# A fourth pair of projection chunks in seven block products, and the gate products in another slot of a sparse-attention layer

## What is computed

```python
h = rmsnorm(x, g_norm)                       # x: 256 x 2048
proj = einsum('bsd,de->bse', h, w_in)        # 2048 -> 4*1024 + 2*1024 + 6*256 + 24 columns
(m_q, m_k, m_v, m_z, n_q, n_kc, n_vc, n_ks, n_vs, n_kw, n_vw, n_g, n_z) = split(proj)
...
q_rot = apply_rope(nq, cos, sin)             # the gated heads' queries, rotated
q_raw = nq                                   # and raw: they meet the compressed keys
k_c = compress_tokens(n_kc, pe_ck, w_ck1, w_ck2)    # silu(flat @ w1) @ w2
v_c = compress_tokens(n_vc, pe_cv, w_cv1, w_cv2)
gates = sigmoid(n_g)                         # three gates per gated head
o_nsa = nsa_attention(q_rot, q_raw, k_c, v_c, k_s, v_s, k_w, v_w, gates)
y = concat([rmsnorm(o_moba * silu(m_z)), rmsnorm(o_nsa * silu(n_z))])
return x + einsum('bse,ed->bsd', y, w_out)
```

## Time and profile before

| | |
|---|---|
| median of 3 runs | 496.52 us (496.51 to 496.88) |
| the profiled execution, its own time | 496.67 us |
| its span (first to last instruction) | 494.9 us |
| around the span | 1.77 us |
| granted TensorE clock, mean | 0.997 |
| PE / DVE / ACT / POOL busy | 98% / 71% / 52% / 13% |
| HBM read and written | 93.93 MB and 2.10 MB |

### The profile page before, as it was taken

How to read it: one execution, slowest core, us unless ns; L and a number is a source line. 1 busy time by engine, 2 the same in 40 slices (tenths; PEclk the granted TensorE clock), 3 DMA queues, 4 the chain that set the end, 5 groups by cost and what they waited for, 6 DMA issues and landing times.

```text
span 494.9 us, 6495 instructions
## 1 busy us (share of the span) xinstructions
PE 485.8 (98%) x2506; PEld 404.2 (82%) x2506; DVE 352.1 (71%) x554; ACT 256.7 (52%) x368; POOL 64.2 (13%) x66
## 2 busy tenths in 40 slices
PE   8999999999999999999999999999999999999993
PEld 7888788787788888888888888888888888888882
DVE  5886643445879958776587887766898879888643
ACT  5884335353556535645444455664665546466422
POOL 2350101000202202000020200000313231040120
PEclk9999999999999999999999999999999999999998
DMA  8989788685454552533544724448247769643304
GB/s 293 329 285 378 248 301 298 200 281 179 148 182 159 166 174 88 170 121 136 171 134 164 255 59 158 141 150 303 85 136 267 277 244 310 230 152 116 140 1 170
DMA packets 54576, 96.45 MB, mean 195 GB/s; under 512 B 4401, under 2 KB 13201, under 8 KB 54161
## 3 DMA queue, kind: packets, MB, share of 16 engines
q1 hardware_dynamic: 54512, 96.03, 57.0%
q10 hardware_dynamic: 32, 0.01, 0.0%
HBM read 93.93 MB, written 2.10 MB: 194 GB/s over the span
## 4 chain that ended last, share of the span: by engine, by line
PE 96%; issue 1%; DMA 1%; DVE 0%; ACT 0%; ACTq 0%; POOLq 0%; POOL 0%; DVEq 0%
PE proj L677 26%; PE proj L679 26%; PE proj L678 26%; PE b_o L974 4%; PE b_t L658 2%; PE b_p L943 2%; PE b_s L843 2%; PE proj L710 2%; PE proj L716 1%; PE proj L721 1%; DMA xo<-in_x_dram 1%; PE b_s L679 1%; PE b_s L677 1%; PE b_s L678 1%; PE b_p L658 0%
## 5 line engine op out<-in xcount | busy, mean ns | idle before, releaser
L1391 DVE TENSOR_TENSOR w_lo<-w_raw,w_hi 128x2048 fp32r<-128x2048 f32 x67 | 155.3, 2320 | 74.6 <-ACT w_hi L1053 74.4
L677 PE MATMUL proj<-w_hi,xT_hi 128*128 128x512 f32 x500 | 197.1, 394 | 0.0
L679 PE MATMUL proj<-w_hi,xT_lo 128*128 128x512 f32 x500 | 195.0, 390 | 0.0
L678 PE MATMUL proj<-w_lo,xT_hi 128*128 128x512 f32 x500 | 194.8, 390 | 0.0
L1053 ACT ACTIVATE w_hi<-w_raw 128x2048 fp32r<-128x2048 f32 x67 | 127.9, 1912 | 27.5 <-PE proj L679 17.0
L677 PEld LDWEIGHTS proj<-w_hi,xT_hi 128*128 128x128 f32 x500 | 93.9, 188 | 20.8 <-issue 1.6
L679 PEld LDWEIGHTS proj<-w_hi,xT_lo 128*128 128x128 f32 x500 | 93.8, 188 | 20.0
L678 PEld LDWEIGHTS proj<-w_lo,xT_hi 128*128 128x128 f32 x500 | 94.0, 188 | 18.5
L1199 ACT ACTIVATE pT<-b_p 128x512 f32<-128x512 f32 (+2 forms) x24 | 11.8, 490 | 53.9 <-PE b_p L943 53.9
L625 POOL TENSOR_TENSOR rope_a<-rope_a,rope_b 128x512 f32<-128x512 f32 (+1 forms) x12 | 13.1, 1108 | 160.8 <-DVE rope_b L1478 160.8
L677 PE MATMUL proj<-w_hi,ymT_hi 128*128 128x512 f32 x70 | 27.3, 390 | 0.0
(11 more groups left out here) (252 smaller groups left out, 562.9 us busy)
## 6 DMA issues: line engine op xcount, KB each, us to landing
w_raw<-in_w_in_dram SPq DMA_DIRECT2D x53, 1024.0 KB, 5.1
w_raw<-in_w_out_dram SPq DMA_DIRECT2D x14, 1024.0 KB, 5.1
xo<-in_w_ck_dram SPq DMA_DIRECT2D x4, 1024.0 KB, 7.8
xo<-in_w_cv_dram SPq DMA_DIRECT2D x4, 1024.0 KB, 7.8
w_raw<-in_w_in_dram SPq DMA_DIRECT2D x12, 256.0 KB, 6.5
Q<-in_x_dram SPq DMA_DIRECT2D x1, 2048.0 KB, 10.1
out_dram<-Q SPq DMA_DIRECT2D x8, 256.0 KB, 2.8
xo<-in_x_dram SPq DMA_DIRECT2D x3, 512.0 KB, 7.6
```

Source lines behind the costliest of these rows:

```text
L677: nc.tensor.matmul(dst, a_hi, b_hi, start=first, stop=False, skip_group_check=goes_on)
L678: nc.tensor.matmul(dst, a_hi, b_lo, start=False, stop=False, skip_group_check=goes_on)
L679: return nc.tensor.matmul(dst, a_lo, b_hi, start=False, stop=last, skip_group_check=goes_on)
L1391: nc.vector.tensor_tensor(wl, w_raw[:, u % RAW], wh.bitcast(F32), ALU.subtract).then_inc(lo_ready, 1)
```

## The change

The two `nq` chunks (3 and 4) become the first pair of four. Their seven block products are spread over slots 10 to 13, and slot 18 has no unit of its own any more. The four fp32 weight blocks and three of the four half-done copies lie in `Q`, where the fp32 transposed x was: so the gates' products, which read it, move from slot 13 to slot 4 (their sums to slot 5, on all engines), and SP waits for them before it loads two of the blocks. The raw queries are finished by DVE (`nq_sums`) and not by ACT. The later pairs keep their slots.

```diff
-PAIRS = [(11, 12), (13, 14), (NC + 2, NC + 3)]
+PAIRS = [(3, 4), (11, 12), (13, 14), (NC + 2, NC + 3)]
+FIRST_BLOCKS, T2_SLOT, EARLY = [8, 40, 48, 65], [10, 41, 49, 66], [10, 42, 50, 66]
+MIDDLE_BLOCKS, LATE_BLOCKS = [11, 42, 50, 67], [12, 43, 51, 68]
+MIDDLE, LATE = [12, 44, 52, 68], [13, 45, 53, 69]
...
+ROUNDED_AT = {9: 10, 10: 11, 11: 12, 12: 13, 13: 14, 14: 15, 15: 16, 17: 17,
...
-CK_LOAD = [6, 7, 11, 12, 14, 15, 17, 18]
+CK_LOAD = [6, 7, 11, 12, 13, 14, 16, 17]
-GATE_SLOT = 13
+GATE_SLOT = 4
...
+                if u == 8:
+                    block(NQ_PAIR, 0)
+                if u == 10:
+                    sp.wait_ge(gates_done, 1)
+                    block(NQ_PAIR, 1)
+                    block(NQ_PAIR, 3)
+                if u == 12:
+                    sp.wait_ge(xs_lo_ok, 1)
+                    block(NQ_PAIR, 2)
...
-                if kv:
-                    pe.wait_ge(gate_exp, 2)
+                pe.wait_ge(gate_exp, 2)
...
-                if slot == 40:
-                    xs_round()
+                if slot in (7, 40):
+                    xs_round((7, 40).index(slot))
...
                     if slot == MIDDLE[p]:
-                        if p == 2:
+                        if p in (NQ_PAIR, OUT_PAIR):
                             block_hi(p, 4)
                             block_hi(p, 5)
                         mid_out_(p, 2)
...
+            def nq_sums(i):
+
+                n = CHUNKS[i][2]
+                dve.wait_ge(unit_used, used_by_chunk(i))
+                dve.wait_ge(mid_out, 4)
+                if n:
+                    dve.wait_ge(t_round, rounds_by(UPC * i + UPC - 1))
+                copies = [mid_copy(NQ_PAIR, c) for c in ((0, 3) if n else (2, 1))]
+                for m in range(MT):
+                    nc.vector.scalar_tensor_tensor(raw_e[:, m, :], proj_b[i % 2][m][:, :], rstd[:, m:m + 1], copies[m],
+                                                   ALU.mult, ALU.add).then_inc(dve_read, 1)
...
-                if slot == 38:
-                    x_sums()
-                if slot == 40:
-                    xs_residual()
+                if slot in (6, 38):
+                    x_sums((6, 38).index(slot))
+                if slot in (8, 40):
+                    xs_residual((8, 40).index(slot))
```

More of the change, by code:

```diff
@@ L75, in plain @@
         units.append((c, g))
[L77 to L93, removed]
+    starts = {pair[0]: p for p, pair in enumerate(X_PAIRS)}
+    for c in range(NC):
+        p = PAIR_OF.get(c)
+        for g in range(UPC):
+            if g == (2 if p is None else 3) and c + 1 in starts:
+                ring.append(("early", starts[c + 1]))
+            if p is None or g:
+                if c in starts and g < 3:
+                    ring.append((("middle", "late")[g - 1], p))
+                plain(c, g)
     for c, g in OUT_UNITS[:-1]:
         plain(NC + c, g)
-    a, b = PAIRS[2]
-    ring.append(("early", 2))
+    a, b = PAIRS[OUT_PAIR]
+    ring.append(("early", OUT_PAIR))
     plain(NC + OUT_UNITS[-1][0], OUT_UNITS[-1][1])
-    ring.append(("middle", 2))
+    ring.append(("middle", OUT_PAIR))
     plain(a, 1)
-    ring.append(("late", 2))
+    ring.append(("late", OUT_PAIR))
     for c, g in ((a, 2), (a, 3), (b, 1), (b, 2), (b, 3)):
@@ L122, in unit_at @@
 def unit_at(slot):
-    for p, (a, b) in enumerate(PAIRS[:Z_PAIRS]):
+    for p, (a, b) in enumerate(X_PAIRS):
         s0 = MIDDLE[p]
@@ L127, in unit_at @@
             return {2: UNIT_NO[a, 2], 3: UNIT_NO[a, 3], 4: UNIT_NO[b, 1], 5: UNIT_NO[b, 2], 7: UNIT_NO[b, 3]}.get(slot - s0)
[L128 to L136, removed]
+    a, b = PAIRS[OUT_PAIR]
+    late = LATE[OUT_PAIR]
+    if slot >= MIDDLE[OUT_PAIR]:
+        return {late + 1: UNIT_NO[a, 2], late + 2: UNIT_NO[a, 3], late + 3: UNIT_NO[b, 1]}.get(slot)
+    if slot >= NPROJ:
+        c, g = OUT_UNITS[slot - NPROJ]
+        return UNIT_NO[NC + c, g]
+    return UNIT_NO[slot // UPC, slot % UPC]
+ROUNDED_AT = {9: 10, 10: 11, 11: 12, 12: 13, 13: 14, 14: 15, 15: 16, 17: 17,
+              41: 40, 42: 41, 43: 42, 44: 43, 45: 44, 46: 45, 47: 46, 49: 47, 50: 48, 52: 49, 53: 50, 54: 51, 55: 52, 56: 53, 57: 54, 58: 55,
+              66: 61, 67: 62, 68: 63, 69: 64, 70: 65, 71: 66, 72: 67}
 def rounded_at(slot):
-    if slot < 40:
+    if slot < 8:
         return slot + 2
-    return slot - 2 if 60 <= slot < 65 else ROUNDED_AT.get(slot)
+    if 18 <= slot < 40:
+        return slot
+    return slot - 4 if 60 <= slot < 65 else ROUNDED_AT.get(slot)
 OUT_SLOT = [OUT_DONE[0], OUT_DONE[1] + 1, OUT_DONE[2]]
@@ L1003, in _ @@
                 for p in range(len(PAIRS)):
-                    if slot == EARLY[p] and p < Z_PAIRS:
+                    if slot == EARLY[p] and p != OUT_PAIR:
                         pair_early(p)
@@ L1360, in _ @@
                     act.wait_ge(gates_sum, 1)
+                    act.wait_ge(rstd_ok, 2)
                     for m in range(MT):
@@ L1788, in _ @@
                         block_lo(p, 1)
-                    if slot == MIDDLE_BLOCKS[p] and p:
+                    if slot == MIDDLE_BLOCKS[p] and p != Z1:
                         block_lo(p, 2)
```

237 lines of the change are left out of this document (124 added, 113 removed).

## The result

The changed kernel takes **499.78 us** (median; its four executions: 499.14, 498.89, 500.42 and 500.52) against 496.69 before: a ratio of 1.0062, 95% interval 1.0049 to 1.0075. That is 3.1 us slower. The forecast was 498.7, with 497.0 to 500.2 as its range. The profiled execution took 499.14 with a span of 497.3, 2.4 above the span of before.

A forecast was written before the change was run, and what follows sets the result against it. PE was taken as the bound, busy 485.8 of 494.9 us. The profiled 496.67 - 1.36 (products) + 1.05 (slots 10 to 13) + 2.45 (slot 18) = 498.81, 0.15 above the median, so 498.7; range 497.0 to 500.2.

The forecast's parts named there:

- Six products, -1.36: Pair of chunks: 42 block products replace 48, six fewer at 0.227 us each, -1.36 us on PE.
- The rival of blocks that switch buffers: Pair's blocks: more frequent buffer switches eat into the six products' gain, 0.2 us at most; no chance of its own.
- Gates moved, 0: Slots 13 and 14 to 4 and 5: PE does the gates' 16 products, 1.73 us, in either place; cost 0.
- Early part, 0: Slots 6 to 10: some 8 us of added DVE work and smaller DMA pieces cost PE nothing.
- Slots 10 to 13, +1.05: Longer ACT and DVE queues make PE wait before P7 (0.6 to 0.7), then 0.25 and 0.15; ends 0 and 2.2.
- Slot 18, +2.45: Second layer directly behind the MLP's sums waits for `hid_ready`: 2.37 us formerly hidden by a unit, plus 0.1 waking.
- the collision: Slot 18: hidden's first DVE step takes 1.11 us beside POOL's addition; without it 0.9 less (rivals 0.10 and 0.07).
- After slot 18, no wait: Slots 19 and 20 onward: PE is nearer to ACT and DVE, yet waits for nothing; cost 0.
- 3.1 us nearer: Slots 19 and 20: second layer begins 2.45 us behind the sums, not 5.54, bringing PE closer to ACT and DVE.
- The clock, 0.03: Rival: slot 18's wait brings on a stretch at granted clock 0.88, costing 1.5 us more, 500.2; chance 0.03.

The follow-up runs named there:

- the half unit and the later sum: Changed kernel with half of slot 19's unit moved into slot 18 before the second layer, and DVE's fourth block sum moved from slot 11 to 12: 497.51 us, ratio 1.0015.
- the half unit: Changed kernel with slot 19's unit cut in two, its first half in slot 18 between the MLP's sums and second layer: 498.69 us, ratio 1.0041.
- the gates alone: Kernel before with only the gates' products and small steps moved from slots 13 and 14 to 4 and 5: 496.81 us, ratio 1.0006.
- the earlier rounding: Changed kernel with ACT's and DVE's rounding of slot 19's unit one slot earlier, in slot 16: 498.52 us, ratio 1.0040.
- the wait alone: Kernel before with only the values' second layer in slot 18 placed ahead of the unit, directly behind the MLP's sums: 500.96 us, ratio 1.0080.
- the best version: Changed kernel with the half unit, later fourth sum, earlier rounding, two more units rounded ahead, and DVE's slot 17 residual before the hidden layer: 495.99 us, ratio 0.9992.

## Why the prediction came out as it did

The direction, the two places and the mechanisms were right; the median of 499.78 is 1.1 above the forecast: 0.6 to 0.9 of it is the clock, 0.3 the gates. That it stayed inside the range is in part luck, since it lies between two shorter and two longer executions; the longer ones (500.42 and 500.52) are outside. The forecast's steps, from the transposes of slot 4 to the second layer in slot 18 (131.18 - 37.61 = 93.57 after, 91.27 before: +2.30):

- *Six products, -1.36.* Right. The blocks cost what the same products cost elsewhere. In the run with the half unit and the later sum nothing waits in slots 11 to 13, and PE took 19.3 us from the end of slot 10's MLP products at 80.5 to the start of slot 13's at 99.8, where the prediction's rates give 18.9. In the kernel before the same stretch took 17.9 where they give 17.55, so the rates are short by the same 0.4 without any block. The rival of blocks that switch buffers falls.
- *Gates moved, 0.* This term was too small: +0.31 in the rows of the gates alone. Nothing waited in that stretch; the products are slower by 0.13 there and the unit behind them by about 0.2. Why, is open.
- *Early part, 0.* Right: no wait of PE on another engine from slot 6 to slot 11.
- *Slots 10 to 13, +1.05.* Measured 1.00. P7 waited 0.36 and stood 0.5 later than without it; the rest are stops too short for the table of waits (0.1 to 0.2 each where the fourth copy and the last block are due).
- *Slot 18, +2.45.* Measured 2.4, with the collision: 1.13 for the first step (forecast 1.11). The run with the earlier rounding shows the 0.9 that the collision is worth.
- The terms give -1.36 + 0.31 + 1.00 + 2.4 = 2.35 for the 2.30 measured.
- *After slot 18, no wait.* True of the changed kernel, by luck. I compared PE with the queues at one place ("3.1 us nearer") and didn't add up DVE's work over the next 45 us, 43.6 busy. It cost nothing only since the wait of slot 18 held PE back; 0.4 us of it appeared with the earlier rounding and 2.1 with the half unit.
- *The clock, 0.03.* This is the step that failed, beside the gates' term. I took it that a wait of this size brings no stretch at the lower clock, since no row showed one, and no row of before could: PE never waited in the middle of the kernel. An absent row bounds nothing. The price that I put on it, 1.5 us and 500.2, was near the 1.4 that the longer executions lost (500.42 and 500.52), though I had it from the tail, which is not where it happens. It struck 2 of 4 executions of the changed kernel and 4 of 5 with the wait alone. The Trainium skill, page TensorE: Matmul & The Clock Gate, section Part 1: The HAM clock gate, has an idle PE fall to 1.2 GHz; the stretch at 127 to 129 agrees, at a granted clock of 0.50.

The collision behaves as the Trainium skill says, page SBUF — State Buffer, section SBUF: two separate sides. By it a DVE instruction with two inputs in SBUF (or in a two-port mode) and a GpSimd instruction that reads SBUF exclude each other, and whichever starts first keeps the shared ports for the whole instruction. Two rows agree. The residual (two inputs) that began 0.05 us before POOL's addition kept its 2.29, and POOL took 3.40; and the hidden layer's first step, which began 0.19 after POOL's addition, ended 0.05 after it (130.28 and 130.23).

Open: why the gates cost 0.3 more in slot 4, why the clock fell in some executions and not in others with the same wait, and whether the 0.4 that the best version gains holds, since its interval just reaches 1.

## What to carry to other kernels

When a unit of cover leaves a slot, price every chain that it hid, then add up the busy time of the engine that the work moved to over the next few slots: here three limits lay behind each other (a latency chain, a queue's order, a full queue), and each fix showed only the next. Here a wait of 2.4 us on PE cost 4.3 to 4.8 us in four executions of five, through the clock, and 2.7 in the fifth; so look at the clock of each execution, not at one profile. Filling a wait with unused matmuls tells waiting and clock apart in one run.

## What the runs showed of the hardware

- After a wait of 2.4 us PE's granted clock fell to 0.50 in 6 of 9 executions by their times and mean clocks (one of them profiled), and products took 0.43 us each; at waits of 1.5 us in none of 9, and with the 2.4 us filled with matmuls in none of 10.
- The four additions of POOL between 128 and 160 us each hold up one instruction of DVE in the changed kernel. For the first the runs without the overlap show it, for the others it is read from the times alone. Its timeline of DVE:

```profile
129.16 1.12 DVE L1552 TENSOR_SCALAR hid_e<-hid_e 128x64 f32<-128x64 f32 x1 [0.27 <-ACT hid_e L1239]
...
136.00 3.38 DVE L1410 TENSOR_TENSOR w_lo<-w_raw,w_hi 128x2048 fp32r<-128x2048 f32 x1
...
151.96 0.96 DVE L1604 TENSOR_TENSOR coef<-coef,gate 128x2 f32<-128x2 f32 x1
...
159.06 1.26 DVE L1601 TENSOR_SCALAR coef<-sums 128x2 f32<-128x2 f32 x1
...
165.23 0.16 DVE L1604 TENSOR_TENSOR coef<-coef,gate 128x2 f32<-128x2 f32 x1
```

  Against 0.20, 2.29, 0.16 and 0.16 for the same forms elsewhere that is 3.9 us, of 43.6 busy. The second of them (3.38) is new with the change: in the kernel before, DVE waited 2.21 us for ACT ahead of the residual in that place.
